# Gate and up projection as seven block products, with the down projection's first operand sums moved ahead of the last gate-up results

## What is computed

```
hn = (_rms(x, norm2_g[l]) * (1 + sc2) + sh2).astype(x.dtype)
gate, up = jnp.split(hn @ w_gate_up[l], 2, axis=-1)
x = x + g2 * ((jax.nn.silu(gate) * up) @ w_down[l])
```

## Time and profile before

| | |
|---|---|
| median of 3 runs | 1439.56 us (1439.05 to 1442.39) |
| the profiled execution, its own time | 1443.05 us |
| its span, first to last instruction | 1441.0 us |
| PE busy | 1401.5 us, 97% of the span |
| DVE busy | 401.8 us, 28% |
| ACT busy | 244.2 us, 17% |
| TensorE clock granted, mean of the span | 0.998 of full speed |
| gate-up stage, first to last product | 1216.0 to 1371.5 us |
| down stage | 1371.5 to 1441.0 us |

### The profile page before, as it was taken

The page is one execution under the profiler, slowest core; times in us unless marked ns, Lnnn a source line. Parts: engine busy times, 40 slices in busy tenths (PEclk is TensorE's granted clock), DMA queues, the critical chain, the costliest instruction groups (busy, mean ns, idle before and its releaser), DMA issues.

```text
span 1441.0 us, 17517 instructions
## 1 busy us (share of the span) xinstructions
PE 1401.5 (97%) x7070; PEld 736.0 (51%) x7070; DVE 401.8 (28%) x968; ACT 244.2 (17%) x444; POOL 0.2 (0%) x4
## 2 busy tenths in 40 slices
PE   8999999999999999999999999999899999999999
PEld 4654444444444443443334333433388765888843
DVE  4766112112111111211111111211223762002684
ACT  3542101101111110111011100101213343000000
POOL 0000000000000000000000000000000000000000
PEclk9999999999999999999999999999999999999999
DMA  9979999999999999999999999999997425544400
GB/s 304 407 309 368 415 428 428 426 427 429 429 428 428 429 428 428 428 429 429 429 428 428 429 427 428 428 429 425 416 370 240 166 88 188 163 148 157 162 1 29
DMA packets 80975, 496.38 MB, mean 344 GB/s; under 512 B 6281, under 2 KB 43862, under 8 KB 53314
## 3 DMA queue, kind: packets, MB, share of 16 engines
q1 hardware_dynamic: 80324, 494.70, 84.5%
q10 hardware_dynamic: 606, 1.06, 0.2%
HBM read 494.68 MB, written 1.05 MB: 344 GB/s over the span
## 4 chain that ended last, share of the span: by engine, by line
PE 74%; DMA 23%; DVE 2%; issue 0%; ACT 0%; SPq 0%; DVEq 0%; ACTq 0%
PE PS L991 19%; DMA ring<-in_w_gate_up_dram 16%; PE PS L1017 11%; PE PS L1393 11%; PE PS L976 6%; PE PS L1135 6%; DMA qk<-in_w_gate_up_dram 5%; PE PS L1403 5%; PE PS L1026 3%; DMA ring<-in_w_ada_dram 2%; PE PS L1259 2%; PE PS L816 2%; PE PS L707 1%; PE PS L686 1%; PE PS L698 1%; PE PS L1003 1%
## 5 line engine op out<-in xcount | busy, mean ns | idle before, releaser
L991 PE MATMUL PS<-ring,store 128*64 128x512 f32 x1360 | 300.9, 594 | 14.0 <-DMA ring<-in_w_gate_up_dram 13.6
L991 PEld LDWEIGHTS PS<-ring,store 128*64 128x64 f32 x1360 | 93.8, 137 | 208.2 <-issue 171.5
L2201 DVE TENSOR_SCALAR store<-PS 128x512 f32<-128x512 f32 x32 | 22.1, 691 | 622.5 <-PE PS L991 622.5
L1017 PE MATMUL PS<-ring,store 128*64 128x512 f32 x704 | 154.8, 592 | 0.0
L1393 PE MATMUL PS<-xc,ring 128*128 128x256 f32 x704 | 152.3, 379 | 0.1
L1393 PEld LDWEIGHTS PS<-xc,ring 128*128 128x128 f32 x704 | 133.7, 190 | 18.9 <-issue 0.8
L976 PE MATMUL PS<-store,rows 128*128 128x64 f32 x1024 | 121.4, 272 | 0.2 <-DVE store L2179 0.2
L976 PEld LDWEIGHTS PS<-store,rows 128*128 128x128 f32 x1024 | 119.7, 192 | 1.1 <-issue 1.1
L1605 ACT ACTIVATE store<-store 128x512 f32<-128x512 f32 x32 | 20.1, 629 | 450.3 <-DVE store L2201 450.3
L1017 PEld LDWEIGHTS PS<-ring,store 128*64 128x64 f32 x704 | 49.4, 137 | 90.7 <-issue 89.0
L1135 PE MATMUL PS<-ring,xc 128*128 128x240 f32 (+1 forms) x448 | 93.9, 366 | 0.1
(11 more groups left out here) (382 smaller groups left out, 1197.6 us busy)
## 6 DMA issues: line engine op xcount, KB each, us to landing
ring<-in_w_gate_up_dram SPq DMA_DIRECT2D x82, 2048.0 KB, 35.0
ring<-in_w_down_dram SPq DMA_DIRECT2D x43, 2048.0 KB, 37.1
qk<-in_w_gate_up_dram SPq DMA_DIRECT2D x20, 2048.0 KB, 37.5
ring<-in_w_gate_up_dram SPq DMA_DIRECT2D x28, 1024.0 KB, 5.1
ring<-in_w_ada_dram SPq DMA_DIRECT2D x24, 1024.0 KB, 16.3
store<-in_w_gate_up_dram SPq DMA_DIRECT2D x11, 2048.0 KB, 34.9
xc<-in_w_down_dram SPq DMA_DIRECT2D x10, 2048.0 KB, 36.4
store<-in_w_down_dram SPq DMA_DIRECT2D x10, 2048.0 KB, 37.8
```

Source lines behind the costliest of these rows:

```text
L991: mm = pe.matmul(bank(b)[CAP * h:CAP * (h + 1), :], xg[:, k, :], w[:, b * FE + h * 512:b * FE + (h + 1) * 512], start=False, stop=(k == KD ...
L1017: mm = pe.matmul(bank(3)[CAP * h:CAP * (h + 1), :], lhs, w[:, (f % 2) * D + h * 512:(f % 2) * D + (h + 1) * 512], start=False, stop=(f == 7))
L2201: v.tensor_scalar(g_min, bank(0), LIMIT, None, ALU.min).then_inc(clipped, 1)
```

## The change

The gate-up stage takes the seven-product scheme too. The tokens are cut in two halves of 128 and the 1024 input features in two halves of 512; the gate chunk and the up chunk are the two column halves of the right operand. A block product is now 128 tokens (stationary, from `cols` or a sum of its blocks) by 256 columns over 512 features: 4 products of 128 x 256, and seven of these, 28 per pair in place of 32. What follows from it:

- `gu_sums(j)` on DVE makes the weight sums of pair j: four instructions of 128 x 1024. For pair 0 it also makes the four sums of the input blocks (128 x 512). Pairs 0 and 1 are done before any result; then `gu_sums(j + 2)` comes after the results of pair j.
- `gate_up_2(j)` on DVE adds the seven products to gate and up and multiplies: nine instructions of 128 x 256. ACT copies the first product out of PSUM and applies silu twice (lines 1905 and 1910).
- The results now have tokens on partitions, so the PE turns them (`turn_h`, four 128 x 128 transposes per pair) and ACT copies the turned tiles to `h_t` (`keep_h`, line 1899). `turn_h(j - 1)` stands behind the third product of pair j; before the seventh product of pair j the PE waits for `h_kept`, which is the copy of pair j - 1. The last pair is turned behind the third down product.
- The gain is spread behind the first two block products of pair 0, into banks 2 and 3.
- On DVE `scale_weights` of chunks 0 to 4 stands behind `gu_sums` of pairs 5 to 9, one each; `seven_sums(0)` and `seven_sums(1)` stand between the results of pair 9 and those of pair 10. From there `seven_sums(i - 3)` and `scale_weights(i)` take turns for i = 5 to 10, and three `seven_sums` end it. The tail of the down stage waits for the scaled chunks first, and for the last sums only ahead of its third product.
- Buffers: the sums of both stages lie in `mod`, `rows`, `qk`, `gfin` and `wide`; the down products use other PSUM banks. Several semaphores are merged or renamed elsewhere (`lat_ready`, `routing_done`, `conv_act`, `ml_act`); the instructions there stay as they are.

```diff
+        GU_FIRST = (0, 1, 2, 5, 6, 3, 4)
+        GU_ORDER = (0, 1, 5, 6, 3, 4, 2)
...
-        SEVEN_BANK = (0, 1, 2, 3, 6, 7, 4)
+        SEVEN_BANK = (0, 1, 2, 4, 5, 6, 3)
...
+            def gu_product(j, m):
+
+                b11, t3, b21, b22, t1, t2, t4 = gu_rows(j)
+                a11, _, a12, a22, s1, s2, s3, s4 = gu_cols()
+                lhs, rhs = ((a11, b11), (a12, b21), (s4, b22), (a22, t4), (s1, t1), (s2, t2), (s3, t3))[m]
+                for k in range(4):
+                    if (j, m) in ((0, 0), (0, 1)):
+                        need_col(4 * m + k)
+                    mm = pe.matmul(gu_bank(j, m), lhs[:, k, :], rhs[:, k * CW:(k + 1) * CW], start=(k == 0), stop=(k == 3))
...
+            def turn_h(j):
+
+                pe.wait_ge(sig["h_ready"], j + 1)
+                if j:
+                    pe.wait_ge(sig["h_kept"], j)
...
             for j in range(PAIRS):
                 if j >= 2:
                     pe.wait_ge(sig["h_ready"], j - 1)
...
+                for i, m in enumerate(gu_order(j)):
+                    if j == 0 and m in (2, 5, 6, 3):
+                        pe.wait_ge(sig["sums_ready"], 1 + (2, 5, 6, 3).index(m))
+                    elif i == 2:
+                        pe.wait_ge(sig["sums_ready"], 4 + j)
+                    elif i == 3:
+                        if j == 1:
+                            pe.wait_ge(sig["bcast_kept"], 2)
+                        turn_h(j - 1)
+                    elif i == 6:
+                        pe.wait_ge(sig["h_kept"], j)
+                    gu_product(j, m)
...
-            pe.wait_ge(sig["sums_ready"], FT // 2)
+            pe.wait_ge(sig["w_scaled"], 4 + FT // 2)
             for m in SEVEN_LAST:
+                if m == 5:
+                    pe.wait_ge(sig["sums_ready"], 3 + PAIRS + FT // 2)
...
             for j in range(PAIRS):
-                act.wait_ge(chunk_used, N_GU2 + 2 * j + 1)
...
-                do.tell(nc.scalar.activation(h_sil[:, j % 2, :], bank(4 + 2 * (j % 2)), ACT.Silu), "silu_ready")
+                h = h_parts[j % 2]
+                act.wait_ge(sig["prod_done"], 3 * j + 1)
+                do.tell(nc.scalar.copy(h[:, 0, :], gu_bank(j, 0)), "silu_ready")
+                for i, part in enumerate((1, 2)):
+                    if i and j:
+                        keep_h(j - 1)
+                    act.wait_ge(sig["gate_sums"], 2 * j + i + 1)
+                    do.tell(nc.scalar.activation(h[:, part, :], h[:, part, :], ACT.Silu), "silu_ready")
...
+            gu_sums(0)
+            gu_sums(1)
             for j in range(PAIRS):
...
+                gate_up_2(j)
...
-                if j >= 6:
-                    scale_weights(N_DN2 + 2 * (j - 6))
-                    scale_weights(N_DN2 + 2 * (j - 6) + 1)
-                if j >= 7:
-                    seven_sums(j - 7)
-            scale_weights(N_END - 1)
-            for i in range(PAIRS - 7, FT // 2):
+                if j + 2 < PAIRS:
+                    gu_sums(j + 2)
+                if 5 <= j < PAIRS - 1:
+                    scale_weights(N_DN2 + j - 5)
+                if j == PAIRS - 2:
+                    seven_sums(0)
+                    seven_sums(1)
+            for i in range(5, FT // 2):
+                seven_sums(i - 3)
+                scale_weights(N_DN2 + i)
+            for i in range(FT // 2 - 3, FT // 2):
                 seven_sums(i)
```

More of the change, by code:

```diff
@@ L374, in two_blocks, with gu_rows, gu_cols, gu_order @@
         h_sil = work[:, FT * T:FT * T + 1024].rearrange("p (b n) -> p b n", b=2)
-        seven_buf = [qk[:, 0:8, :].rearrange("p a b -> p (a b)"), qk[:, 8:16, :].rearrange("p a b -> p (a b)"),
-                     rows[:, :, :].rearrange("p a b -> p (a b)"), cols[:, :, :].rearrange("p a b -> p (a b)")]
+        h_parts = [work[:, FT * T:FT * T + 1024].rearrange("p (b n) -> p b n", b=4),
+                   spare.rearrange("p (b n) -> p b n", b=4)]
+        qk_flat, rows_flat = (x_[:, :, :].rearrange("p a b -> p (a b)") for x_ in (qk, rows))
+        gu_diff = [(qk_flat[:, 0:1024], qk_flat[:, 1024:2048], qk_flat[:, 2048:3072]),
+                   (qk_flat[:, 3072:4096], rows_flat[:, 0:1024], rows_flat[:, 1024:2048])]
+        def gu_rows(j):
+            gate, up = (chunk(N_GU2 + 2 * j + u) for u in range(2))
+            b11, b21, b12, b22 = (w[:, k:k + 4, :].rearrange("p k n -> p (k n)") for w in (gate, up) for k in (0, 4))
+            return (b11, b12, b21, b22) + gu_diff[j % 2]
+        def gu_cols():
+            a11, a12, a21, a22 = (cols[:, k:k + 4, t * P:(t + 1) * P] for t in range(NT) for k in (0, 4))
+            sums = [x_[:, a:a + 512].rearrange("p (k t) -> p k t", k=4) for x_ in (gfin, wide) for a in (0, 512)]
+            return (a11, a21, a12, a22, *sums)
+        GU_FIRST = (0, 1, 2, 5, 6, 3, 4)
+        GU_ORDER = (0, 1, 5, 6, 3, 4, 2)
+        GU_HALVES = {0: (0, 0), 1: (0, 1), 5: (1, 0), 6: (1, 1), 3: (2, 0), 4: (2, 1), 2: (3, 0)}
+        def gu_order(j):
+            return GU_ORDER if j else GU_FIRST
+        def gu_bank(j, m):
+            b, half = GU_HALVES[m]
+            return bank(4 * (1 - j % 2) + b)[:, half * T:(half + 1) * T]
+        def turn_bank(j):
+            return bank(7 if j % 2 else 3)
+        def gu_chunk(j):
+            return (3, gu_order(j)[-1])
+        def gu_tell(j):
+            return (1, 6, 4) if j else (1, 2, 6)
+        seven_buf = [mod[:, :, :].rearrange("p a b -> p (a b)"), rows_flat, qk_flat[:, 2048:4096], qk_flat[:, 0:2048]]
         def seven_rows(i):
```

120 lines of the change are left out of this document (72 added, 48 removed).

## The result

| | before | after |
|---|---|---|
| median | 1439.74 us (8 runs, 1439.05 to 1442.39) | 1432.74 us (8 runs, 1428.62 to 1434.47) |
| ratio of the runs, 95% interval | | 0.9942 (0.9933 to 0.9951) |
| profiled execution, its own time | 1443.05 us | 1428.62 us |
| its span | 1441.0 us | 1426.8 us |
| PE, DVE, ACT busy | 1401.5, 401.8, 244.2 us | 1384.5, 493.2, 257.3 us |

The change gains 7.0 us by the medians and 8.3 us by the ratio, which goes by the means: 0.5 to 0.6%. The forecast was 1431.2 us within 1427.5 to 1435.6, and faster. The profiled execution of after is the fastest of its eight. 4.1 us of its distance to the trace of before lie ahead of the first gate-up product, where the change merges semaphores and leaves the instructions as they are; so I compare from that product on: 225.0 us before, 214.9 us after, **-10.1 us**.

What follows compares the result with a forecast made beforehand. The prediction took PE work to bound the changed stages. Its terms, -19.0 + 4.8 + 0.3 + 0.4 + 3.4 + 0 + 1.7 = -8.4 us, took the median 1439.56 to 1431.2 us, range 1427.5 to 1435.6.

Steps and rivals of the forecast that it cites:

- Products saved: Gate-up stage on PE: 44 fewer products of 128 x 256 at 0.432 us each, -19.0 us.
- Turns added: Gate-up results on PE: 44 transposes of 128 x 128 at 0.11 us each, +4.8 us.
- the turns do not overlap: Rival: added transposes cost 0.276 us each, +12.1; total -1.1, 1438.5 us, no change; chance 0.05.
- Start: Gate-up start: first product group needs four input tiles, all made by DVE, slower than PE uses them; +0.3 us.
- Pairs 6 to 9: Gate-up, ahead of the seventh product: DVE and ACT chain with a scaling just meets PE, 0.1 each, +0.4 us.
- Pair 10: Last gate-up pair: two sets of down sums make the chain 14.2 us against 10.8; PE waits +3.4 us.
- Down stage: 77 products as before; DVE's last sums at 53.3 us, wanted at 53.7; taken as 0 (0 to 0.5).
- The margin of 0.4: Down stage: DVE's last sums due at 53.3 us after pair 10, PE wanting them at 53.7.
- The clock: Behind pair 10's wait: clock expected to fall to half speed for 3.4 us, +1.7 us (0 if none).
- the clock does not fall: Rival: no fall behind pair 10's wait, total -10.1, 1429.5 us; chance 0.22.
- DVE paces the pairs: Rival: DVE's 128 x 256 instructions cost 0.57 us, not 0.42; +3.0 over pairs 6 to 10, 1434.6 us; chance 0.10.
- DVE's handover: Rival: short dependent DVE instructions each cost 0.1 us more, +13.4; total +5.0, 1444.6 us; chance 0.05.

Runs made afterwards that it cites:

- turns_twice: Changed kernel with each group of four turns issued twice, 44 transposes more; 1434.25 us, ratio 0.9958 to the kernel before.
- copy_first: Changed kernel with ACT's copy of the previous pair's turned tiles ahead of the first silu, not behind it; 1429.72 us, ratio 0.9931 to the kernel before.
- after_again: The changed kernel, unedited, timed once more; 1429.8 us (6 runs), ratio 0.9934 to the kernel before.
- experiment 7: The changed kernel, unedited, timed again (1429.8 us) and traced in three further executions (1432.4, 1431.74, 1431.14 us) to see whether the clock falls.
- before_look: The kernel before, unchanged, one more trace; 1442.06 us, 225.0 us from the first gate-up product to the end.
- planned_again: The same kernel as planned, timed once more; 1426.93 us, ratio 0.9907 to the kernel before.
- look_1: The changed kernel, unedited, first of three further traced executions; 1432.4 us.
- planned: Changed kernel with early copy as in copy_first, first down sums behind pair 6, chunk 4 scaled behind pair 8; 1426.47 us, ratio 0.9904 to the kernel before.
- look_2: The changed kernel, unedited, second of three further traced executions; 1431.74 us.
- sums_behind: Changed kernel with both sets of down sums behind the results of pair 10, not ahead; 1435.18 us, ratio 0.9966 to the kernel before.

## Why the prediction was right

Its total and its parts held, with one term that is a chance and not a price.

- **Products saved, -19.0.** 12.09 us for 56 instructions is the price of the earlier trace rows, 0.216. Held.
- **Turns added, +4.8.** 44 x 0.109. Held to 0.01 us each; the upper end of 0.276, which is the rival "the turns do not overlap", is refuted by turns_twice.
- **Start, +0.3.** The first 16 instructions took 4.08 us where 16 x 0.216 = 3.45. Before, the first 64 took 14.05 us where 13.81 are due, so 0.24 was lost there already. That leaves +0.39. Held within the 0 to 0.4 given. That the spread covers the sums of pair 0 held too; without that cover the price is 1.8 us, where I had named only the first wait, 0.7.
- **Pairs 6 to 9, +0.4.** No wait at all. **Pair 10, +3.4:** 3.04 us of idle time, 3.3 with what comes beside it. Both have one cause: I had taken 0.3 us from PE to DVE and 0.1 for each of three handovers more; the chain shows 0.1 for the first (1340.77 to 1340.87) and about 0.15 for the three together. (My 0.3 ran from the first column of the next product, which starts 0.16 ahead of the last result.) The chain of pair 10 is 13.8 us (1340.77 to 1354.60) and not 14.2. That of pair 9 is 10.4 us and not 10.8: its copy ends at 1338.64, 0.2 us ahead of the product group that waits for it (1338.87). The place, the releaser and the reason of the wait are as forecast.
- **Down stage, 0.** 70.39 against 69.53: 0.44 is the turns of pair 10 (in the +4.8), 0.4 lies behind the last instruction of DVE, in the landing of the final output (2.90 us, before 2.48). The product's spacing did not change, so no sums were late. The margin of 0.4 was thin indeed: in copy_first, where the PE comes 3.3 us earlier, it waits 1.3 and 0.6 us. DVE's only idle time between the results of pair 9 and the tail was 0.99 us, at the end of pair 10.
- **The clock, +1.7.** This is the term that was mis-sized, in the step "so I expect a fall". Of five traces of the changed kernel two have a fall, of 3.4 and of 6.8 us, which cost 1.7 and 3.0 us; three have none. The mean of the five is +0.9. (In the batch of the result five of eight executions had a mean clock of 0.997 or less, so falls were more frequent there than in these traces, but it is not shown that they lay behind this wait.) What I set against it, that the PE was dense before this wait, carries more weight than I gave it: the earlier trace rows had falls behind 1.96 and 1.58 us in thin work, while in dense work 2.60 us left none (one trace). The rival "the clock does not fall", -10.1, is exactly what the profiled execution shows: 214.9 - 225.0.

The gate-up stage was forecast at 145 to 146 us and took 144.55: the waits of pairs 6 to 9 are missing, and that of pair 10 is 0.4 us short.

In measured time: my sum gave -8.4; by the ratio the first batch has -8.3 (-9.6 to -7.1) and after_again -9.5 (-11.4 to -7.8), by the medians -7.0 and -10.0. That the first ratio meets the sum to 0.1 us is luck. The traces add up to -10.1 without a fall and to -9.2 with the mean of the five; that the first batch lies at -8.3 fits its four executions at a clock of 0.996 (experiment 7), but no trace of one of them exists. Over all 17 timed executions of the changed kernel the times run from 1428.21 to 1434.47 us with a median of 1431.14. The traces reach only up to 1432.4: no fall and an early start of gate-up (1211.9) gave 1428.62, no fall and a late start (1214.4) 1431.14, two falls, one at 1180 us and one behind the wait of pair 10, and a start at 1213.9 gave 1432.4.

The other rivals fell: each of the new DVE instructions of 128 x 256 takes 0.42 us also where it reads PSUM (line 2604: 425 ns), and the gaps between them are 0.03 us, so neither "DVE paces the pairs" nor "DVE's handover" had any ground.

What stays open: why the part ahead of gate-up takes between 1211.5 and 1216.6 us in 14 traces, in which its instructions are the same. Falls of the clock around 1040 us are in before, before_look, planned_again, copy_first and turns_twice, and one at 1180 us in look_1; but traces without any fall in this part also start gate-up between 1211.5 and 1215.3 us (after_again, planned), so the falls are not all of it. The change only merges semaphores in this part. Both traces of before start gate-up later (1216.0 and 1215.0) than all five of the changed kernel (1211.5 to 1214.4); whether that is chance no run here separates.

## What to carry to other kernels

When work of one engine is moved ahead to fill its idle time, look for the in-order queue behind it: here one copy, whose input had been ready for 7.6 us, stood behind an instruction that waited for the moved work, and it alone made the 3 us wait. Put what is ready ahead of what waits. Then check where the removed wait had been giving some engine its margin: taking it away alone gained 0.9 of 3.3 us, and only together with an earlier place for the DVE work did it gain all of it.

## What the runs showed of the hardware

- At a wait of the PE in dense work the granted clock can fall in one execution and not in the next, with the same code and the same wait: none of 1.29, 1.98 and 2.60 us (one trace each) had a fall; of six waits of 3.04 to 3.05 us three had one; 3.87 and 5.81 us (one trace each) had one. The falls lasted 3.4 or 6.8 us at 1.2 GHz. Those of 3.4 us cost 1.4 to 1.7 us. That of 6.8 us in look_2 cost 3.0, since 0.7 us of it lay within the wait; in sums_behind half of it lay within the wait.
- DVE keeps its speed in such a fall (128 x 512 in 0.69 us, sums_behind), so the fall gives a DVE-bound tail a margin: 0.4 us of wait where 2.5 was reckoned.
- PE idle time of 3.04 us costs 3.3: 0.16 for the overlap that is lost with the next product, and 0.1 for the group behind it, which takes 1.83 us to the start of the next one in place of 1.73.
